# Applying a norm before or behind the products: scaled residual as the operand, the root multiplied into PSUM

## The chip, the core and the metric
One core of a Trainium2 chip (trn2) runs the whole program. The metric is the device time in microseconds of one execution, the median over several runs.

## The reference, cut to what matters
Two layers of a hybrid backbone on 640 tokens: 128 prompt tokens (columns 0 to 127) and 512 sample tokens, each group with its own modulation. Every layer is a mixer followed by a feed-forward part, and ahead of each stands a norm over the 1024 features:

```python
h = rms_norm(x) * P['norm_mix'][layer] * (1 + sc1) + sh1
x = x + g1 * mixer(h)
h = rms_norm(x) * P['norm_ffn'][layer] * (1 + sc2) + sh2
x = x + g2 * conv_ffn(h, ...)       # silu(a) * val of dwconv3(h @ w_up), then @ w_down
```

With gain = norm * (1 + sc) this is h = gain * x * r + sh, where r is one number per token. So h @ W = r * ((gain * x) @ W) + sh @ W. The feed-forward part has 2816 hidden features, a convolution over three neighbouring tokens (not across the two groups) and a bias. Layer 0 mixes by retention and a state-space scan, layer 1 by attention (qkv).

## The kernel before
Activations lie with features on the 128 partitions (eight tiles) and the 640 tokens as columns. A *unit* is one tile of 128 output features: its weights are loaded by SyncE into `raw` (four buffers), ScalarE rounds them to `w_hi` (`act_split`), and another engine makes `w_lo = raw - w_hi` (`low_split`). TensorE (`pe_tile`, L379) makes three products per tile of the contraction (w_hi with the high part, w_lo with the high part, w_hi with the low part of the operand), each in two halves of 320 columns: 48 products in a unit with eight tiles, 42 in one with seven. Two PSUM pairs (`pj`) alternate, and TensorE waits for the reading of the unit before the last (`pj_read0/1`) and for `w_lo`. `w_hi` and `w_lo` have two buffers each.

Each engine has its instructions in one written order, tied by semaphores. The stages in order: modulation A, dt, xs, bc, z, qk, v, g, wo_ssm, wo_ret, then for layer 0 up00, dn00, up01, dn01, up02, dn02 (16 up units and 8 down units, then 14 and 8 twice), kk, q, vv, attention, wo, and up10 to dn12.

Five norms: norm00, normS, norm01 (ahead of up00), norm10 (ahead of kk), norm11 (ahead of up10). All but normS are *wide*. For a wide norm ScalarE squares the tiles of x, VectorE adds them, TensorE sums over partitions (`pe_wide`, L684) with some filler products (`pe_keep`, L678), ScalarE takes the root (`act_root`, L730), VectorE the reciprocal (L742), TensorE spreads it over the partitions (`pe_spread`, L717). Then, tile by tile, VectorE multiplies x by gain and root (L773), ScalarE adds the shift and rounds to `h_hi` (L829), VectorE makes `h_lo` (L783). TensorE begins two units of the next stage interleaved in the order `SKEW`.

In an up unit ScalarE reads PSUM twice, into `u_sb` (L845) and, scaled and with bias, into `t_sb` (L846). VectorE adds the neighbours in two passes, each with a small piece across the chunk edges (L859, L860, L862, L863). Every second unit ScalarE takes the silu (L964), VectorE multiplies (`hf`, L980), ScalarE rounds to `hid_hi` (L966), VectorE makes `hid_lo` (L982). In a down unit VectorE adds the gated result to x (L895, three pieces), and in the last stage ahead of a norm the squares follow (L654, L664).

VectorE also computes the modulation vectors of the later stages in 80 units of four multiply-adds of 512 columns (L564, L567); behind every fourth stands a flip (two transposes L575, a reduce L577). Units 0 to 21 lie in qk to g, 22 to 27 in wo_ssm, 28 to 34 in wo_ret, and 35 to 79 in the feed-forward of layer 0: one behind every second up unit, three more in up01, one behind each unit of dn00 and dn01 and behind four of dn02.

Of the kernel before, what the change touches and what calls it, by code (L numbers as in the profile page):

```python
# [22 lines left out]
HALF = TOK // 2  # L23
COL = [0, 128, 256, 384, 512]
# [60 lines left out]
def build(nc, a, o):  # L85
# [55 lines left out]
    with ctx:  # L141
# [36 lines left out]
        hf2 = sb("hf2", [128, 2, TOK])  # L178
        u_sb = sb("u_sb", [128, 2, TOK])
# [94 lines left out]
        A = Region(A0, A_BYTES)  # L274
        Q2 = A("Q2", [128, AH, TOK], F32R)
# [15 lines left out]
        rope = Region(A0 + 65536, 2048)("rope", [128, 2, 4, 64])  # L291
# [79 lines left out]
        def pe_tile(pe, s, r, k, i, f, X, low=None, high=None):  # L371

            for n, (w, v) in enumerate(((w_hi, X[0]), (w_lo, X[0]), (w_hi, X[1]))):
                if n == 2 and low:
                    pe.wait_ge(*low)
                for hh in range(2):
                    if high and n == 0:
                        pe.wait_ge(*high[hh])
                    last = pe.matmul(pj(f)[:, hh, :], w[:, i % 2, k * 128:(k + 1) * 128], v[:, k, hh * HALF:(hh + 1) * HALF],  # L379
                                     start=(k == 0 and n == 0), stop=(k == s.K - 1 and n == 2))  # L380
            return last

        def pe_unit(pe, s, r, j, X, used=None):
# [5 lines left out]
            for k in range(s.K):  # L389
# [5 lines left out]
        SKEW = ((0, 0), (1, 0), (0, 1), (1, 1), (0, 2), (0, 3), (1, 2), (0, 4), (0, 5), (1, 3), (0, 6), (0, 7),  # L395
                (1, 4), (1, 5), (1, 6), (1, 7))

# [9 lines left out]
        def pe_first(pe, units, X, ready):  # L407
# [4 lines left out]
            elif ready[0] == "hid_ready":  # L412
                m = 4 if units[0][0].name[:3] == "dn0" else 2
                steps = [(0, k) for k in range(K - 1)] + [(1, k) for k in range(m)] + [(0, K - 1)] + [(1, k) for k in range(m, K)]
            else:
                steps = LATER if units[0][0].name == "wo_ssm" else SKEW
            for n, k in steps:
                s, r = units[n]
                if k == 0:
                    pe_begin(pe, s, r)  # L420
                low = high = None
                if n == 0:
                    low = (S(ready[0]), ready[1] + k + 1)
                    if ready[0] == "h_ready" and k == 0 and APPLIED[ready[1] // KT] in WIDE:
                        high = (S("h_hi_a"), WIDE.index(APPLIED[ready[1] // KT]) + 1), (S("h_hi"), ready[1] + 1)
                    elif ready[0] == "h_ready":
# [3 lines left out]
                last = pe_tile(pe, s, r, k, s.u0 + r, s.f0 + r, X, low, high)  # L430
# [21 lines left out]
        H, HID = (h_hi, h_lo), (hid_hi, hid_lo)  # L452
# [57 lines left out]
        def act_modA(act):  # L510
            for k in range(KT):
# [4 lines left out]
                if k == 6:  # L516
# [11 lines left out]
                    "modD": (48, 96, ((1, 0), (1, 1)))}  # L528
# [96 lines left out]
        WIDE = [p for p in NORMS if p != "normS"]  # L625
# [61 lines left out]
        def pe_wide(pe, name):  # L687
# [9 lines left out]
            if i:  # L697
                pe_keep(pe, flat[:, 2048:2560], (192,))
            pe.wait_ge(S("sq_a"), WIDE.index(name) + 1)
            pe_square_sum(pe, 0, sq[:, 1, :], False, True).then_inc(S("ms"), 1)  # L700
            if i:
                pe_keep(pe, flat[:, 2048:2560], (128,))
            pe.wait_ge(S("sq"), KT * (i + 1))
            pe_square_sum(pe, 1, sq[:, 1, :], False, True).then_inc(S("ms"), 1)
            if i:
                pe_keep(pe, flat[:, 2048:2560], (256,))

        def pe_spread(pe, name):
# [3 lines left out]
            if name in WIDE:  # L712
# [6 lines left out]
                if STEP0[name]:  # L719
                    pe_keep(pe, B6, (256, 128))  # L720
# [118 lines left out]

        def act_conv_in(act, s, r, j, cw):  # L840

            c = s.c0 + r
            if c >= 2:
# [3 lines left out]
                           scale=cw[:, r + 4 * j, 1:2] if isinstance(j, int) else cw[:, ds(r + 4 * j, 1), 1]).then_inc(tp_read(s, r), 1)  # L847

# [39 lines left out]
        PIECES = [(0, 0, 0, 128, 0), (1, 0, 128, HALF, 128), (1, 1, 0, HALF, HALF)]  # L888

        def dve_residual(dve, s, r, gate, first=False):  # L890
            evac_wait(dve, s, r, 0)
            out = pj(s.f0 + r)
            for g, hh, a0, a1, c0 in PIECES:
                xs_ = x[:, r, c0:c0 + a1 - a0]
                ins = dve.scalar_tensor_tensor(xs_, out[:, hh, a0:a1], gate(r, g), xs_, MUL, ADD)  # L895
                if first and g and not hh:
                    ins.then_inc(S("res_a"), 1)
            ins.then_inc(tp_read(s, r), 1)

        def act_out_stage(act, s, norm=None, hooks={}):  # L900
            for r in range(s.M):
# [14 lines left out]
        EARLY = 28  # L916
# [1665 lines left out]
```

## Time and profile before

| | |
|---|---|
| median of 3 runs | 1963.88 us (1961.39 to 1965.11) |
| profiled execution, first to last instruction | 1963.8 us |
| TensorE / VectorE / ScalarE / GpSimd busy | 97% / 65% / 42% / 6% |
| mean granted clock of TensorE | 0.994 |
| HBM read, mean rate | 170 MB, 89 GB/s |

Products overlap, so that a busy TensorE doesn't tell how fast it works: the distance of two starts does. A timeline row merges like instructions; in brackets is the engine's idle time just before and who ended it. A windows row gives, for each engine, busy time and count, then TensorE's granted clock, the DMA share and GB/s.

### The profile page before, as it was taken

The page shows a single profiled execution, that of the slowest core. Times are in us where ns is not written, and L with a number is a line of the kernel's source. Part 1 is how long each engine was busy: PE and PEld are TensorE (multiplying, and loading weights), DVE is VectorE, ACT ScalarE, POOL GpSimd, SP SyncE. Part 2 cuts the span into 40 slices and gives each one's busy share as a digit, 9 for nine tenths or more (in the row PEclk, how much of TensorE's full clock was granted, in tenths as well). Part 3 has the DMA queues.
Part 4 walks back from the last instruction along what each step waited for, and adds up shares of the span by engine and source line. Part 5 has one row for each costly group of instructions (what it writes and reads, how often), then busy time and mean ns, then how long its engine had stood idle before and what let it go on. Part 6 is the DMA issues. An engine that isn't in the chain of part 4 may idle for free.

```text
span 1963.8 us, 33247 instructions
## 1 busy us (share of the span) xinstructions
PE 1899.8 (97%) x13415; PEld 1803.0 (92%) x13415; DVE 1267.7 (65%) x2101; ACT 818.5 (42%) x1367; POOL 119.6 (6%) x106
## 2 busy tenths in 40 slices
PE   7999999999998999999999999899999999999999
PEld 4998799999988899999999989866698999999999
DVE  5555944666877878878978876656536553553553
ACT  4645743222444355234234345555525541441441
POOL 0000200000020000000000026411100000000000
PEclk9999999999999999999999999999999999999999
DMA  8221012445311333433433322100012222222222
GB/s 309 86 77 39 13 60 87 150 137 155 114 57 62 122 107 118 144 125 117 161 131 103 109 90 67 57 1 1 1 54 65 75 66 84 75 67 77 73 69 78
DMA packets 57066, 175.96 MB, mean 90 GB/s; under 512 B 7553, under 2 KB 9473, under 8 KB 56833
## 3 DMA queue, kind: packets, MB, share of 16 engines
q1 hardware_dynamic: 55152, 172.17, 27.3%
q10 hardware_dynamic: 1808, 2.36, 0.3%
q8 instruction: 69, 1.13, 0.3%
q14 instruction: 37, 0.30, 0.0%
HBM read 170.05 MB, written 4.46 MB: 89 GB/s over the span
## 4 chain that ended last, share of the span: by engine, by line
PE 83%; DVE 9%; ACT 4%; issue 2%; DMA 1%; POOL 1%; SPq 0%; ACTq 0%; DVEq 0%; POOLq 0%
PE ps L379 69%; PE ps L2117 2%; PE ps L2102 2%; DVE t_sb L773 1%; DVE w_lo L368 1%; DVE h_lo L783 1%; ACT w_hi L360 1%; PE ps L880 1%; PE ps L1295 1%; DVE PT L2234 1%; PE ps L2070 1%; PE ps L2069 1%; DVE x L895 1%; PE ps L1282 1%; DMA modw<-in_w_modA 1%
## 5 line engine op out<-in xcount | busy, mean ns | idle before, releaser
L379 PE MATMUL ps<-h_hi,w_hi 128*128 128x320 f32 x2768 | 638.6, 312 | 9.0 <-DVE w_lo L368 3.2
L379 PE MATMUL ps<-h_lo,w_hi 128*128 128x320 f32 x2768 | 633.7, 310 | 9.4 <-DVE h_lo L783 8.2
L379 PE MATMUL ps<-h_hi,w_lo 128*128 128x320 f32 x2768 | 630.8, 309 | 0.0
L368 DVE TENSOR_TENSOR w_lo<-raw,w_hi 128x1024 fp32r<-128x1024 f32 (+1 forms) x218 | 268.0, 1230 | 449.3 <-ACT w_hi L360 449.1
L360 ACT ACTIVATE w_hi<-raw 128x1024 fp32r<-128x1024 f32 (+1 forms) x221 | 230.7, 1044 | 694.1 <-PE ps L379 693.9
L379 PEld LDWEIGHTS ps<-h_lo,w_hi 128*128 128x128 f32 x2768 | 462.2, 188 | 16.5 <-DVE h_lo L783 14.9
L379 PEld LDWEIGHTS ps<-h_hi,w_hi 128*128 128x128 f32 x2768 | 461.1, 188 | 16.7 <-issue 5.2
L379 PEld LDWEIGHTS ps<-h_hi,w_lo 128*128 128x128 f32 x2768 | 463.4, 188 | 0.0
L379 PE MATMUL ps<-hid_hi,w_hi 128*128 128x320 f32 x704 | 161.7, 311 | 3.8 <-DVE x L895 2.8
L379 PE MATMUL ps<-hid_hi,w_lo 128*128 128x320 f32 x704 | 160.8, 309 | 0.0
L379 PE MATMUL ps<-hid_lo,w_hi 128*128 128x320 f32 x704 | 160.7, 309 | 0.0
L379 PEld LDWEIGHTS ps<-hid_hi,w_hi 128*128 128x128 f32 x704 | 117.8, 188 | 5.9 <-issue 2.6
L379 PEld LDWEIGHTS ps<-hid_hi,w_lo 128*128 128x128 f32 x704 | 118.3, 188 | 0.0
L379 PEld LDWEIGHTS ps<-hid_lo,w_hi 128*128 128x128 f32 x704 | 118.2, 188 | 0.0
L567 DVE SCALAR_TENSOR_TENSOR maccB<-mrawB,csil,maccB 128x512 f32<-128x512 f32 x168 | 115.3, 746 | 0.0
L895 DVE SCALAR_TENSOR_TENSOR x<-ps,modT,x 128x128 f32<-128x128 f32 (+2 forms) x216 | 81.3, 432 | 14.0 <-PE ps L379 14.0
L2089 DVE TENSOR_REDUCE nmax<-ps 128x1 f32<-128x640 f32 (+1 forms) x80 | 57.1, 715 | 38.1 <-PE ps L2070 38.0
L966 ACT ACTIVATE hid_hi<-hf 128x640 f32 (+1 forms) x44 | 32.6, 740 | 112.2 <-DVE hf L980 112.2
L846 ACT ACTIVATE t_sb<-ps,fconv 128x640 f32<-128x640 f32 x88 | 77.3, 878 | 0.0
L863 DVE SCALAR_TENSOR_TENSOR t_sb<-u_sb,fconv,t_sb 128x635 f32<-128x635 f32 x88 | 76.9, 874 | 0.0
L860 DVE SCALAR_TENSOR_TENSOR t_sb<-u_sb,fconv,t_sb 128x635 f32<-128x635 f32 x88 | 76.9, 874 | 0.0
L845 ACT ACTIVATE u_sb<-ps 128x640 f32<-128x640 f32 x104 | 71.5, 687 | 2.2 <-PE ps L379 2.2
(285 smaller groups left out, 2008.0 us busy)
## 6 DMA issues: line engine op xcount, KB each, us to landing
raw<-in_ffn_up SPq DMA_DIRECT2D x88, 512.0 KB, 3.6
raw<-in_hyb_in SPq DMA_DIRECT2D x49, 512.0 KB, 3.8
mrawB<-in_w_modB SPq DMA_DIRECT2D x48, 512.0 KB, 4.3
mrawA<-in_w_modB SPq DMA_DIRECT2D x64, 256.0 KB, 2.8
raw<-in_ffn_down SPq DMA_DIRECT2D x32, 448.0 KB, 3.3
raw<-in_hyb_out SPq DMA_DIRECT2D x16, 512.0 KB, 4.2
raw<-in_ffn_down SPq DMA_DIRECT2D x16, 512.0 KB, 3.5
modw<-in_w_modA SPq DMA_DIRECT2D x12, 512.0 KB, 13.2
```

What stands on the lines that cost most here:

```text
L360: act.activation(w_hi[:, i % 2, 0:n], raw[:, b % RAW, 0:n], ACT.Copy).then_inc(S("w_hi"), 1)
L368: eng.tensor_tensor(w_lo[:, i % 2, 0:n], raw[:, b % RAW, 0:n], w_hi[:, i % 2, 0:n].bitcast(F32), SUB).then_inc(S("w_lo"), 1)
L379: last = pe.matmul(pj(f)[:, hh, :], w[:, i % 2, k * 128:(k + 1) * 128], v[:, k, hh * HALF:(hh + 1) * HALF], start=(k == 0 and n == 0), sto ...
L567: ins = dve.scalar_tensor_tensor(acc, w, c, acc, MUL, ADD)
L845: act.activation(two(u_sb[:, r % 2, :]), pj(s.f0 + r), ACT.Copy).then_inc(S("cv_u"), 1)
L846: act.activation(two(t_sb[:, r % 2, :]), pj(s.f0 + r), ACT.Identity, bias=cw[:, r + 4 * j, 3:4] if isinstance(j, int) else cw[:, ds(r + 4 ...
L860: dve.scalar_tensor_tensor(t[:, :, 1:128], u[:, :, 0:127], w(0), t[:, :, 1:128], MUL, ADD).then_inc(S("cv_mid"), 1)
L863: dve.scalar_tensor_tensor(t[:, :, 0:127], u[:, :, 1:128], w(2), t[:, :, 0:127], MUL, ADD).then_inc(S("cv_done"), 1)
L895: ins = dve.scalar_tensor_tensor(xs_, out[:, hh, a0:a1], gate(r, g), xs_, MUL, ADD)
L2089: dve.tensor_reduce(nmax[:, n % 4:n % 4 + 1], score(n), AX.X, MAX, negate=True).then_inc(S("at_m"), 1)
L2102: last = pe.transpose(TP[:, b, :], Pr[n % 3][:, b * 128:(b + 1) * 128], ident)
L2117: last = pe.matmul((B6, B7)[u % 2][64 * par:64 * par + 64, 0:256].rearrange("p (m t) -> p m t", m=2), v, PT[:, u % 2, b - b0, par:AR:2, :] ...
```

## The change
For norm01, norm10 and norm11 the operand of the products becomes gain * x (high part by ScalarE in `act_scaled`, low part by VectorE in `dve_scaled`), made within the units of the stage ahead. The shifts of both groups are two extra columns (128 and 129), so operands have 642 columns, in pieces of 322 and 320; the hidden tiles keep these columns too. The sum over features is taken with one-column products (`pe_ms`) within the first unit and the root is spread within the second (`pe_spread` without its wide part); ScalarE copies it into `rstd` (`act_rstd`). VectorE multiplies each unit's PSUM by `rstd` (`dve_product`), ScalarE adds the shift column in two pieces (`act_shifted`) and then makes `up_t` from `up_u`; the convolution is two passes without small pieces. The two first units of a stage run one after the other. All `low_split` are VectorE's now. Four modulation units move from wo_ret to the z stage (EARLY 28 to 32); the modulation sums for layer 1 are split in two (modD, modE); the load of the retention state and some regions of SBUF move.

```diff
+        def act_scaled(act, name, k):
+            l, w = LAYER_OF[name]
+            for g, c0, c1, at in APART:
+                ins = act.activation(XS[name][0][:, k, at:at + c1 - c0], x[:, k, c0:c1], ACT.Copy, scale=gains[:, l, w, k, g:g + 1])
+            ins.then_inc(S("h_hi"), 1)
+        def dve_product(dve, s, r, j=0):
+            evac_wait(dve, s, r, j)
+            dve.wait_ge(S("prod_free"), PROD0[s.name] + r + 4 * j)
+            dve.tensor_tensor(prod[:, 0:2 * MID].rearrange("p (h c) -> p h c", h=2), pj(s.f0 + r, MID),
+                              rstd[:, 0:2 * MID].rearrange("p (h c) -> p h c", h=2), MUL).then_inc(tp_read(s, r), 1)
+        def act_shifted(act, s, r, j, out, to):
+            act.wait_ge(tp_read(s, r), (s.f0 + r) // 2 + 1 + 2 * j)
+            for (c0, c1), b, at in zip(((0, 128), (130, GAP)), (128, 129), to):
+                ins = act.activation(out[:, at:at + c1 - c0], prod[:, c0:c1], ACT.Identity, bias=prod[:, b:b + 1])
+            ins.then_inc(S("prod_free"), 1)
+        def act_up_in(act, s, r, j, cw):
+            c = s.c0 + r
+            act.wait_ge(S("cv_done"), c - 1 + 4 * j)
+            act_shifted(act, s, r, j, up_u[:, r % 2, :], (0, 130))
+            act.wait_ge(*shifted(s, r, j))
+            act.activation(up_t[:, r % 2, 0:GAP], up_u[:, r % 2, 0:GAP], ACT.Identity, bias=..., scale=...).then_inc(S("up_in"), 1)
+        def dve_up_conv(dve, s, r, j, cw):
+            c, p, n = s.c0 + r, r % 2, GAP - 1
+            dve.wait_ge(S("up_in"), c - stages["up00"].c0 + 1 + 4 * j)
+            u, t = up_u[:, p, :], up_t[:, p, :]
+            dve.scalar_tensor_tensor(t[:, 1:n + 1], u[:, 0:n], w(0), t[:, 1:n + 1], MUL, ADD).then_inc(S("cv_mid"), 1)
+            dve.wait_ge(S("cv_mid"), c + 1 + 4 * j)
+            dve.scalar_tensor_tensor(t[:, 0:n], u[:, 1:n + 1], w(2), t[:, 0:n], MUL, ADD).then_inc(S("cv_done"), 1)
...
             def body(r, j):
+                dve_product(dve, s, r, j)
                 low_split(dve, s.u0 + r + 2, j)
-                dve_conv(dve, s, r, j, cw)
+                dve_up_conv(dve, s, r, j, cw)
...
-        LATE = [("wo_ret", r) for r in range(7)]
+        LATE = [("wo_ret", r) for r in range(3)]
...
-            pe_wide(pe, "norm01")
-            pe_spread(pe, "norm01")
...
```

## Rows read from the trace of the kernel before

**Rows 1.** The page: busy times of the engines, and the chain by engine.
```profile
PE 1899.8 (97%) x13415; PEld 1803.0 (92%) x13415; DVE 1267.7 (65%) x2101; ACT 818.5 (42%) x1367; POOL 119.6 (6%) x106
...
PE 83%; DVE 9%; ACT 4%; issue 2%; DMA 1%; POOL 1%; SPq 0%; ACTq 0%; DVEq 0%; POOLq 0%
```
**Rows 2.** Timeline of ScalarE in up02: start, duration, instruction, idle before.
```profile
1067.74 1.06 ACT L360 ACTIVATE w_hi<-raw 128x1024 fp32r<-128x1024 f32 x1 [4.44 <-PE ps L379]
...
1070.06 0.74 ACT L964 ACTIVATE t_sb<-t_sb 128x640 f32<-128x640 f32 x1
...
1074.78 1.06 ACT L360 ACTIVATE w_hi<-raw 128x1024 fp32r<-128x1024 f32 x1 [0.71 <-PE ps L379]
```
**Rows 3.** Windows over norm01, norm10 and norm11, with two units behind each.
```profile
666.16:691.19 25.03, 22.05 (x170) 18.30 (x169) 19.56 (x43) 14.56 (x27) 2.37 (x1) 1.00 0.13 43
1149.61:1174.08 24.47, 21.96 (x171) 18.48 (x171) 20.34 (x44) 12.98 (x25) 2.36 (x1) 1.00 0.09 23
1483.60:1508.50 24.90, 21.97 (x171) 18.28 (x170) 19.34 (x40) 14.60 (x27) 2.36 (x1) 1.00 0.08 23
```
**Rows 4.** Windows within up01 and within up10.
```profile
857.00:954.00 97.00, 97.00 (x663) 97.00 (x662) 83.28 (x127) 40.27 (x54) 0.00 (x0) 1.00 0.39 126
1508.50:1560.00 51.50, 51.50 (x351) 51.50 (x352) 31.24 (x47) 28.04 (x34) 0.00 (x0) 1.00 0.26 82
```
**Rows 5.** Timeline of TensorE at the start of dn01 and dn02.
```profile
960.02 0.56 PE L379 MATMUL ps<-hid_hi,w_hi 128*128 128x320 f32 x2 [0.73 <-DVE x L895]
...
1110.19 0.67 PE L379 MATMUL ps<-hid_hi,w_hi 128*128 128x320 f32 x2 [2.06 <-DVE x L895]
1110.66 0.73 PE L379 MATMUL ps<-hid_hi,w_lo 128*128 128x320 f32 x2
```
**Rows 6.** Timeline of VectorE at the end of dn02 and in norm10.
```profile
1145.39 1.12 DVE L895 SCALAR_TENSOR_TENSOR x<-ps,modT,x 128x128 f32<-128x128 f32 x3
...
1155.05 1.00 DVE L773 SCALAR_TENSOR_TENSOR t_sb<-x,gains,ps 128x128 f32<-128x128 f32 x2
```
**Rows 7.** Timeline of TensorE around the sums of normS.
```profile
329.48 1.17 PE L672 MATMUL ps<-cst,ssq 128*128 128x1 f32 x10
330.51 0.54 PE L379 MATMUL ps<-h_hi,w_hi 128*128 128x320 f32 x2
```
**Rows 8.** Timelines: VectorE in the retention part, ScalarE in norm10.
```profile
556.69 0.81 DVE L1777 TENSOR_TENSOR PTr<-ps,mTf 128x640 f32<-128x640 f32 x1
...
1164.02 1.01 ACT L829 ACTIVATE h_hi<-t_sb,modT 128x128 fp32r<-128x128 f32 x2 [0.95 <-DVE t_sb L773]
```
**Rows 9.** Timeline of VectorE in an odd unit of up01.
```profile
877.00 1.22 DVE L368 TENSOR_TENSOR w_lo<-raw,w_hi 128x1024 fp32r<-128x1024 f32 x1
...
878.27 0.87 DVE L860 SCALAR_TENSOR_TENSOR t_sb<-u_sb,fconv,t_sb 128x635 f32<-128x635 f32 x1
879.18 0.23 DVE L862 SCALAR_TENSOR_TENSOR t_sb<-u_sb,fconv,t_sb 128x3 f32<-128x3 f32 x1
...
880.30 0.83 DVE L980 TENSOR_TENSOR hf<-t_sb 128x640 f32<-128x640 f32 x1
882.03 0.83 DVE L982 TENSOR_TENSOR hid_lo<-hf,hid_hi 128x640 fp32r<-128x640 f32 x1 [0.91 <-ACT hid_hi L966]
```
**Rows 10.** Timeline of VectorE in up01: a modulation unit with its flip.
```profile
868.77 2.73 DVE L567 SCALAR_TENSOR_TENSOR maccB<-mrawB,csil,maccB 128x512 f32<-128x512 f32 x4
...
873.89 1.22 DVE L368 TENSOR_TENSOR w_lo<-raw,w_hi 128x1024 fp32r<-128x1024 f32 x1
```
**Rows 11.** Windows behind two waits of TensorE.
```profile
1112.00:1116.00 4.00, 4.00 (x23) 4.00 (x23) 4.00 (x8) 0.74 (x1) 0.00 (x0) 0.77 0.61 220
...
1203.00:1208.00 5.00, 3.97 (x28) 3.97 (x29) 4.37 (x5) 1.59 (x3) 1.67 (x2) 1.00 0.34 107
```
**Rows 12.** Timeline of TensorE in the qkv stage.
```profile
1204.03 0.77 PE L1893 MATMUL ps<-cst,rt 128*128 128x128 f32 x5 [1.63 <-POOL rt L1884]
```
**Rows 13.** DMA issues: KB each, median us from issue to landing.
```profile
hf<-in_s_ret ACTq DMA_DIRECT2D x1, 512.0 KB, 5.4
```

More of the change, by code:

```diff
@@ L23 @@
 HALF = TOK // 2
+GAP = TOK + 2
 COL = [0, 128, 256, 384, 512]
@@ L405, in pe_begin, with pe_first @@
                 pe.wait_ge(S(f"pj_read{f % 2}"), f // 2)
-        def pe_first(pe, units, X, ready):
+        def pe_first(pe, units, X, ready, norm=None):
             K = units[0][0].K
@@ L414, in pe_first @@
                 steps = [(0, k) for k in range(K - 1)] + [(1, k) for k in range(m)] + [(0, K - 1)] + [(1, k) for k in range(m, K)]
+            elif norm:
+                steps = [(0, k) for k in range(K)] + [(1, k) for k in range(K)]
             else:
-                steps = LATER if units[0][0].name == "wo_ssm" else SKEW
+                steps = LATER
             for n, k in steps:
+                if norm and (n, k) == (0, 5):
+                    pe_ms(pe, norm, tp_base[norm])
+                if norm and (n, k) == (1, 1):
+                    pe_spread(pe, norm)
                 s, r = units[n]
@@ L450, in tp_full @@
             eng.wait_ge(S("tp_full"), t + 1)
-        H, HID = (h_hi, h_lo), (hid_hi, hid_lo)
+        HALVES = (0, HALF), (HALF, TOK)
+        MID = HALF + 2
+        H, ATTN = (h_hi, h_lo, HALVES), (ya_hi, ya_lo, HALVES)
+        XS = {p: t + (((0, MID), (MID, GAP)),) for p, t in (("norm01", (ya_hi, ya_lo)), ("norm10", (ya_hi, ya_lo)), ("norm11", (yh_hi, yh_lo)))}
+        HIDS = [t + (((0, MID), (MID, GAP)),) for t in ((yh_hi, yh_lo), (ya_hi, ya_lo))]
         QUARTER = (0, 2, 1, 3)
@@ new lines, in dve_scaled, with act_rstd @@
+        def dve_scaled(dve, name, k):
+            l, w = LAYER_OF[name]
+            dve.wait_ge(S("h_hi"), KT * APPLIED.index(name) + k + 1)
+            for g, c0, c1, at in APART:
+                ins = dve.scalar_tensor_tensor(XS[name][1][:, k, at:at + c1 - c0], x[:, k, c0:c1], gains[:, l, w, k, g:g + 1],
+                                               XS[name][0][:, k, at:at + c1 - c0].bitcast(F32), MUL, SUB)
+            ins.then_inc(S("h_ready"), 1)
+        def act_rstd(act, name):
+            act_root(act, name)
+            tp_full(act, tpf_base[name])
+            for g, c0, c1, at in APART:
+                ins = act.activation(rstd[:, at:at + c1 - c0], flat[:, 2048 + c0:2048 + c1], ACT.Copy)
+                if not g:
+                    continue
+                ins.then_inc(S("tp_read"), 1)
+            for at in (128, GAP):
+                ins = act.activation(rstd[:, at:at + 2], ones[:, 0:2], ACT.Copy)
+            ins.then_inc(S("prod_free"), 1)
@@ new lines, in build @@
+        PROD0, c = {}, 0
+        for n, names in enumerate((("up00", "up01", "up02"), ("kk", "q", "vv"), ("up10", "up11", "up12"))):
+            for t in names:
+                PROD0[t] = n + 1 + c
+                c += stages[t].M
+        def dve_product(dve, s, r, j=0):
[3 more added lines that the diff above has]
+                              rstd[:, 0:2 * MID].rearrange("p (h c) -> p h c", h=2), MUL).then_inc(tp_read(s, r), 1)
@@ L885, in dve_T, with pieces, dve_residual @@
             dve.tensor_copy(dst, TP).then_inc(S("tp_read"), 1)
-        PIECES = [(0, 0, 0, 128, 0), (1, 0, 128, HALF, 128), (1, 1, 0, HALF, HALF)]
-        def dve_residual(dve, s, r, gate, first=False):
+        def pieces(s):
+            at = 130 if s.name[:2] == "dn" else 128
+            return [(0, 0, 0, 128, 0), (1, 0, at, at + HALF - 128, 128), (1, 1, 0, HALF, HALF)]
+        def dve_residual(dve, s, r, gate):
             evac_wait(dve, s, r, 0)
-            out = pj(s.f0 + r)
-            for g, hh, a0, a1, c0 in PIECES:
+            out = pj(s.f0 + r, MID)
+            for g, hh, a0, a1, c0 in pieces(s):
                 xs_ = x[:, r, c0:c0 + a1 - a0]
                 ins = dve.scalar_tensor_tensor(xs_, out[:, hh, a0:a1], gate(r, g), xs_, MUL, ADD)
-                if first and g and not hh:
-                    ins.then_inc(S("res_a"), 1)
             ins.then_inc(tp_read(s, r), 1)
@@ L2448, in _ @@
             pool_ret(pool)
-            low_split(pool, stages["wo_ret"].u0 + 9)
             pool_tables(pool)
-            low_split(pool, stages["dn02"].u0 + 9)
             pool_rope(pool)
             pool_att(pool)
-            low_split(pool, stages["wo"].u0 + 9)
         @block.tensor
```

233 lines of the change are left out of this document (131 added, 102 removed).

## The prediction
> **What bounds the kernel now.** I read the page's busy shares first, then its chain, then three kinds of stretch. TensorE is busy 97% of the span, VectorE 65%, and the chain that ended last lies on TensorE for 83% and on VectorE for 9% [rows 1]. So a change gains only what it takes out of TensorE's queue or of TensorE's waits. Where it runs undisturbed a unit takes 7.04 us from one split of ScalarE to the next (1067.74 to 1074.78) [rows 2]: 48 products, 0.1467 us each.
>
> The reader is then to see two places. First, the borders: from the last product before a wide norm to the third unit behind it pass 25.03, 24.47 and 24.90 us [rows 3], in which TensorE has two units (14.08 us) of the new stage. 10.95, 10.39 and 10.82 us, 32.2 in all, are the norm: sums of squares, spread, kept-warm products, and waits of 0.8 us for h_lo. Second, the feed-forward of layer 0. There VectorE is nearly full already: 83.3 of 97.0 us between 857 and 954, against 31.2 of 51.5 in layer 1 [rows 4]. TensorE waited for it where up goes over into down: twice at dn01, 0.73 us each (the later stands), and 2.06 us at dn02 [rows 5].
>
> **The change, part by part.** I sum against the profiled execution, 1963.8 us from first to last instruction; the median of the runs is 1963.88, so no correction.
>
> *Borders.* Scaled residuals are made unit by unit, so only the last of eight tiles is late. After the last product at T: residual 1.12, square-add 0.8, scaling 1.0 like L773, square-add 0.8, scaling 1.0 on VectorE [rows 6], so the last h_lo comes at about T+4.8, and TensorE asks for it at T+7. The second unit's w_lo comes at about T+6 and is asked for at T+8. No wait is left. The old interleaving, pe_wide, pe_keep and the 16 spread products go. In their place come five sums (L672) and five spreads (L723), each five in 1.03 us up to the next product, 1.12 with that one's slower start, as L672 stands in the qk stage; the spread, which writes more columns, I take as the same [rows 7]: 2.24 per border, 6.7 in all. The product of unit 0 must wait for the root: spread at T+10.4, ScalarE's copies to T+11.8, product done T+12.7, w_lo of unit 2 T+13.9; TensorE wants both at T+16. Hidden with 2 us to spare. Net -32.2+6.7 = -25.5 (bounds -28 and -20: spread half as dear, or a wait of 2 us at each border).
>
> *Columns.* 2 more per pair of products, in 100 up and qkv units (24 pairs) and 48 down units (1056 pairs): 3456 pairs. A product is 0.1467 us for 320 columns, so at most 0.46 ns per column, at least 0.42 if part is fixed: +3.0 us (2.9 to 3.2).
>
> *Feed-forward, layer 0.* A product on VectorE comes ahead of every unit, and the convolution loses its two small pieces. The new thing is not the busy time but a relay: VectorE multiplies, ScalarE adds the shift in two pieces, waits for itself and makes up_t, and only then may VectorE convolve. Before, both ScalarE readings of PSUM could run ahead while VectorE was late. Costs: the product like PTr, 0.81; two ScalarE pieces (128 and 512) 1.01 from the first's start to the second's end; up_t like L964, 0.74 [rows 8, 2]. Hand-overs are 0.03 to 0.14 us: hid_hi and two of them fill 0.91 around its 0.74 [rows 9]; 0.05 each, with 0.08 for the wait on itself, is my estimate. From product to convolution 2.75 us. low_split (1.22, and 1.13 to the next start, since VectorE starts an instruction some 0.08 before the last one's end) fits inside and hides; 0.8 of the relay is idle. The convolution: 0.91 to its second half (878.27 to 879.18); that, 0.80 where nothing waits for it and 0.98 where the next waits for its end (1.12 from 879.18, less 0.14 for the small piece). Even unit: 2.75+1.71 = 4.5 us (was 1.13+0.14+0.91+0.14+0.80 = 3.1). Odd unit: 2.75+0.91+0.98, then 1.73 from hf to hid_lo, 0.75 for that = 7.1 us [rows 9]. A modulation unit adds 2.65 (2.73 less the 0.08); every fourth also the flip, 2.47, since both take 5.12 (868.77 to 873.89) [rows 10]. A pair with its modulation unit is 14.3 us; TensorE's pair is 14.08+0.04. VectorE had about 2.3 us to spare in a pair without flip and now has none.
>
> What lag L (VectorE's start on an even unit, behind TensorE's end of it) costs nothing? The w_lo of unit r+2 comes at L+2.1 and is wanted at 7.06, so L up to 4.9. After each pair L becomes max(7.06, L+4.5)+9.8-14.12, that is 2.7 from rest, and L+0.15 later; a flip adds 2.47. up00 (flips at r=1 and 9): 5.2 after the first pair, wait 0.3; three pairs at 0.13; second flip, wait 2.6. Sum 3.4, and 0.2 in dn00. up01 has three extra modulation units and three flips: VectorE needs about 117.8 us for what TensorE does in 98.8. Carried over the stage and dn01 by the same rule: waits of 0.4, 0.1, 2.7, 1.2, 2.7, then 2.9, 0.5 and 1.1 in dn01, sum 11.7. up02 and dn02: 0.9, then 1.0 and 3.6 at the start of dn02 (flip in the last pair), 0.1: 5.6. All: 20.9. The same carrying with the costs of before gives 0.9, 1.2 and 2.1 in the two down stages, 4.5 with small ones, against the measured 0.73, 0.73 and 2.06 [rows 5]; so the rule is trusted to about 0.3 per wait.
>
> *Clock.* Behind its wait of 2.06 us TensorE's first two products took 0.47 us and the next ones 0.53 per two, against 0.29, to 1113.9: at 1.2 instead of 2.4 GHz, 1.4 us lost, and a granted clock of 0.77 from 1112 to 1116. Behind 1.63 us at 1204 the clock stayed 1.00 [rows 5, 11, 12]. Five waits above are over 2 us: 5 x 1.4, against 1.4 before, +5.6; part is paid twice, since a late TensorE lets VectorE catch up, and the carrying has counted that within up01. Feed-forward 0: 20.9-4.5+5.6 = +22. Bounds: +3 if ScalarE's leg hid altogether (VectorE's busy time alone), +14 with 0.15 us less per relay, +29 with 0.2 us more.
>
> The Trainium skill (TensorE: Matmul & The Clock Gate, HAM oscillation) says that a kernel whose array waits again and again can be throttled anew behind each wait. [rows 11] agree for 2.06 us and not for 1.63; by that rule alone, with all waits over 1 us counted, the term would be about 5 us larger.
>
> *Feed-forward, layer 1.* No modulation units: pairs take 4.5+7.1 = 11.6 of 14.1 us. The hidden tiles come 0.1 us later for each down stage: +0.2.
>
> *QKV.* Product and wider ScalarE copy hide in the steady part. At its start TensorE already waits for the rope chain, 1.63 us at the third flip [rows 12]. Behind the K flips VectorE goes straight on, so each product (0.75) sits in that chain, three times: +2.5 us (0 to 6, the upper with a clock drop and a late start of attention).
>
> *At nothing, or nearly.* Four modulation units move into the z stage, where VectorE has a low_split, a product and a square-add, 1.2+0.8+0.8 us of each 7.04; 2.65 more fit, and the w_lo of the next unit stands ahead of them in the queue; their loads keep their distance of about three units. If that cover were gone a unit would cost 2.65. The state load moves two hooks later: issued at about 547.7 by my reckoning (7.04 us per unit, flip at r=5), landing 5.4 us later, first asked for ahead of the mask at 556.69; cover 3.6 us [rows 13, 8]. The two mod sums: one extra group on TensorE, +0.3. The POOL low_split leaves the border.
>
> Sum: -25.5+3.0+22+0.2+2.5+0.3 = +2.5, so **1966.3 us**.
>
> **The rivals.** *Relay overlaps (faster).* If ScalarE's leg falls under low_split or runs in less than I take, VectorE keeps its spare time in up01 and the waits stay near 3 to 10. For it: ScalarE is only 42% busy [rows 1], and 0.8 us of idle per relay decides all. Against it: the hand-overs in [rows 9] leave little to shave. Time: 1966.3-19 = 1947 to 1966.3-9 = 1957. It decides below 3.9 us per even unit.
> *VectorE costs more (slower).* The product reads two PSUM banks while ScalarE and TensorE use others; 0.2 us more per relay gives +7, a longer qkv chain +3, clock drops of 2 us instead of 1.4 +3: about 1979. It decides above 4.7 us per even unit.
> *The borders don't close.* A wait on the last scaled tile or the root of over 3 us each would leave 10 of the 25: 1976. Against it stands the slack of 2 us worked out above. This includes that the change fails to do its work.
>
> **How the numbers follow.** Forecast 0.55, with its own range 1959 to 1974; relay overlaps 0.20; VectorE dearer 0.17; borders 0.08. A measurement here can tell 0.2%, 3.9 us, from no change. Faster: 0.20 and 0.05 of the forecast's lower end, 0.25. Same: 0.30, all of it the forecast. Slower: 0.20 of the forecast's upper end with 0.17 and 0.08, 0.45. Range 1952 to 1984: it leaves out the lower half of the overlap case and the ends of the slower two.
>
> **What would show it.** Borders: from the last product to the third unit 16.3 us, instead of 25. up00, up01 and up02: TensorE waiting for w_lo (low_split) with single waits of 2.5 to 3 us behind flips, most in up01, VectorE over 95% busy or in short waits for ScalarE there, product to convolution 2.75 us. Layer 1: no waits, unit 7.06 us. Granted clock below 1.00 behind the long waits. Wrong if up01 shows less than 5 us of waits, if its relay is under 2.3 us, or if TensorE waits at the borders.

## The result and the profile after

The changed kernel takes 1983.85 us (median of 5, 1982.65 to 1986.82), the kernel before in the same session 1965.11 (1961.39 to 1966.03): ratio 1.0114, 95% interval 1.0102 to 1.0125. It is slower: by 19 us between these two medians, by 22 us by the ratio (the kernel before took 1961.6 to 1961.9 beside most later runs). I had forecast 1966.3, no measurable change, though I had given "slower" the largest chance, 0.45; the time lies at the very end of the range. The profiled execution spans 1985.0 us, 21.2 more than that of before.

The page of the changed kernel, busy times and the chain by engine (answers to [rows 1]):

```profile
PE 1904.7 (96%) x13261; PEld 1814.5 (91%) x13261; DVE 1303.7 (66%) x1986; ACT 865.4 (44%) x1476; POOL 114.0 (6%) x103
...
PE 71%; DVE 14%; ACT 8%; issue 6%; DMA 1%; POOL 1%; ACTq 0%; SPq 0%; DVEq 0%; POOLq 0%
```

VectorE's and ScalarE's share of the chain has grown from 13% to 22% and "issue" from 2 to 6: somewhere TensorE now follows these two. Where, the distance between equal marks tells. ScalarE splits the weights of the same 221 units in both kernels, and each split (but for the first two of a stage) starts when TensorE is done with the unit two before. Taking the start of each split in both traces gives how much each stage grew:

| stretch | growth, us | by the prediction |
|---|---|---|
| all up to wo_ret's last units | +0.1 | +0.3 |
| three borders | -8.40, -8.09, -8.09: -24.6 | -25.5 |
| up00 / dn00 | +8.70 / +0.45 | layer-0 stages in all: |
| up01 / dn01 | +18.11 / 0.00 | +22, and |
| up02 / dn02 | +6.52 / +2.31 | columns of 1.4: |
| these six | +36.1 | +23.4 |
| qkv with attention | +3.9 | +2.8 |
| wo | +0.6 | 0 |
| layer 1, feed-forward | +4.8 | +1.6 |
| first split and rounding | +0.3 | |

The borders, TensorE from the first product on gain * x to that of the third unit; the three rows answer to [rows 3]:

```profile
666.21:682.69 16.48, 16.48 (x118) 16.48 (x117) 8.49 (x15) 7.99 (x14) 0.00 (x0) 1.00 0.23 69
1177.35:1194.32 16.97, 16.97 (x124) 16.96 (x122) 8.61 (x15) 6.56 (x15) 0.00 (x0) 1.00 0.17 52
1507.74:1524.20 16.46, 16.46 (x119) 16.46 (x117) 8.34 (x15) 7.99 (x14) 0.00 (x0) 1.00 0.13 37
```

16.3 had been forecast; TensorE is busy throughout. What is left of the norm stands in TensorE's timeline as two groups of small products, 1.03 us each to the next product, as taken from [rows 7]:

```profile
670.69 1.17 PE L682 MATMUL ps<-cst,ssq 128*128 128x1 f32 x10
671.72 0.54 PE L387 MATMUL ps<-ya_hi,w_hi 128*128 128x322 f32 x2
...
675.34 1.28 PE L720 MATMUL ps<-cst,rs 128*128 128x128 f32 x10
676.37 0.54 PE L387 MATMUL ps<-ya_hi,w_hi 128*128 128x322 f32 x2
```

The loss lies in the feed-forward of layer 0. All that TensorE waited for between 679 and 1180 us (waits view: engine, line, who ended the wait; us in total, times, longest):

```profile
PE ps L387 <- DVE w_lo L375: 19.9, 12, 4.2
PE ps L387 <- DVE x L995: 4.5, 2, 3.9
PE ps L387 <- DVE yh_lo L1094: 1.0, 2, 0.5
```

That is 25.4 us, against 4.1 in these stages before. The largest, in TensorE's timeline:

```profile
760.66 0.56 PE L387 MATMUL ps<-ya_hi,w_hi 128*128 128x322 f32 x2 [3.00 <-DVE w_lo L375]
...
909.69 0.63 PE L387 MATMUL ps<-ya_hi,w_hi 128*128 128x322 f32 x1 [2.74 <-DVE w_lo L375]
927.14 0.56 PE L387 MATMUL ps<-ya_hi,w_hi 128*128 128x322 f32 x2 [1.61 <-DVE w_lo L375]
944.20 0.56 PE L387 MATMUL ps<-ya_hi,w_hi 128*128 128x322 f32 x2 [2.52 <-DVE w_lo L375]
...
968.74 0.90 PE L387 MATMUL ps<-yh_hi,w_hi 128*128 128x322 f32 x2 [4.19 <-DVE w_lo L375]
...
1137.77 0.66 PE L387 MATMUL ps<-yh_hi,w_hi 128*128 128x322 f32 x2 [3.86 <-DVE x L995]
```

VectorE in two units of up01 that follow one another (start, duration; the last row begins the next unit). It answers to [rows 9]:

```profile
907.60 0.82 DVE L898 TENSOR_TENSOR prod<-ps,rstd 128x644 f32<-128x644 f32 x1
908.34 1.22 DVE L375 TENSOR_TENSOR w_lo<-raw,w_hi 128x1024 fp32r<-128x1024 f32 x1
910.74 0.89 DVE L938 SCALAR_TENSOR_TENSOR up_t<-up_u,fconv,up_t 128x641 f32<-128x641 f32 x1 [1.18 <-ACT up_t L928]
911.66 0.89 DVE L940 SCALAR_TENSOR_TENSOR up_t<-up_u,fconv,up_t 128x641 f32<-128x641 f32 x1
912.46 0.82 DVE L898 TENSOR_TENSOR prod<-ps,rstd 128x644 f32<-128x644 f32 x1
...
915.54 0.89 DVE L938 SCALAR_TENSOR_TENSOR up_t<-up_u,fconv,up_t 128x641 f32<-128x641 f32 x1 [1.13 <-ACT up_t L928]
...
919.20 0.83 DVE L1094 TENSOR_TENSOR yh_lo<-up_m,yh_hi 128x642 fp32r<-128x642 f32 x1 [0.91 <-ACT yh_hi L1073]
919.94 2.73 DVE L581 SCALAR_TENSOR_TENSOR maccB<-mrawB,csil,maccB 128x512 f32<-128x512 f32 x4
```

From product to convolution pass 3.14 and 3.08 us, and VectorE stands idle for 1.18 and 1.13 of them. An even unit is 4.86 us (907.60 to 912.46), an odd one 7.48 (912.46 to 919.94). The forecast had 2.75, 4.5 and 7.1. ScalarE's side of the same kind of relay shows where the difference is:

```profile
881.27 1.02 ACT L905 ACTIVATE up_u<-prod 128x128 f32<-128x128 f32 x2 [1.67 <-DVE prod L898]
882.54 0.93 ACT L928 ACTIVATE up_t<-up_u,fconv 128x642 f32<-128x642 f32 x1 [0.24 <-ACT up_u L905]
```

up_t takes 0.93 us and not the 0.74 of L964, which has neither scale nor bias vector, and ScalarE stands idle for 0.24 us behind its own shift and not 0.08. A row of the right form stood in the trace of the kernel before, just ahead of the one that I took (ScalarE in up02):

```profile
1069.29 0.88 ACT L846 ACTIVATE t_sb<-ps,fconv 128x640 f32<-128x640 f32 x1
```

It reads PSUM and not SBUF, but has scale and bias as vectors, and takes 0.88 us. The Trainium skill (ScalarE: Activation LUTs, What ACT_TABLE_LOAD costs) gives 186 ns and 0.833 ns per element for an instruction with immediate scale and bias, and about 93 ns more for each of the two that is a vector. My estimate from these figures is 0.91 us for up_t; the row shows 0.93.

### The profile page after: what moved, and what is told of

The parts are those of the page before. It is cut to its first block, busy times and chain, and to the rows that moved or that the text cites. A ratio compares the mean times of both kernels' runs of the same rounds, so it can differ in the third digit from the quotient of the medians.

```text
span 1985.0 us, 33178 instructions
## 1 busy us (share of the span) xinstructions
PE 1904.7 (96%) x13261; PEld 1814.5 (91%) x13261; DVE 1303.7 (66%) x1986; ACT 865.4 (44%) x1476; POOL 114.0 (6%) x103
## 4 chain that ended last, share of the span: by engine, by line
PE 71%; DVE 14%; ACT 8%; issue 6%; DMA 1%; POOL 1%; ACTq 0%; SPq 0%; DVEq 0%; POOLq 0%
PE ps L387 58%; PE ps L2221 2%; PE ps L2236 2%; ACT up_t L928 2%; DVE maccB L581 2%; ACT up_u L905 2%; DVE up_t L938 2%; DVE prod L898 2%; DVE up_m L1092 1%; DVE up_t L940 1%; PE ps L978 1%; PE ps L2189 1%; DVE PT L2353 1%; ACT yh_hi L1073 1%; PE ps L1407 1%
## 5 line engine op out<-in xcount | busy, mean ns | idle before, releaser
L387 PE MATMUL ps<-ya_hi,w_hi 128*128 128x322 f32 (+1 forms) x1376 | 321.3, 315 | 16.0 <-DVE w_lo L375 15.0
L387 PE MATMUL ps<-ya_hi,w_lo 128*128 128x322 f32 (+1 forms) x1376 | 317.2, 312 | 0.0
L387 PE MATMUL ps<-ya_lo,w_hi 128*128 128x322 f32 (+1 forms) x1376 | 316.7, 312 | 0.0
L387 PE MATMUL ps<-yh_hi,w_hi 128*128 128x322 f32 (+1 forms) x1056 | 244.3, 312 | 10.5 <-DVE w_lo L375 4.9
L387 PEld LDWEIGHTS ps<-ya_hi,w_hi 128*128 128x128 f32 x1376 | 231.1, 190 | 20.7 <-issue 18.7
L387 PE MATMUL ps<-h_hi,w_hi 128*128 128x320 f32 x1040 | 241.8, 314 | 7.3 <-DVE w_lo L375 2.8
L387 PE MATMUL ps<-h_lo,w_hi 128*128 128x320 f32 x1040 | 238.4, 310 | 2.5 <-DVE h_lo L780 1.3
L387 PE MATMUL ps<-h_hi,w_lo 128*128 128x320 f32 x1040 | 237.7, 310 | 0.0
L387 PEld LDWEIGHTS ps<-h_hi,w_hi 128*128 128x128 f32 x1040 | 173.2, 189 | 12.2 <-DVE w_lo L375 4.9
L387 PEld LDWEIGHTS ps<-h_lo,w_hi 128*128 128x128 f32 x1040 | 174.4, 189 | 3.8 <-DVE h_lo L780 2.2
L387 PEld LDWEIGHTS ps<-h_hi,w_lo 128*128 128x128 f32 x1040 | 174.5, 189 | 0.0
```

Source lines behind the costliest of these rows:

```text
L387: last = pe.matmul(pj(f, c1 - c0)[:, hh, :], w[:, i % 2, k * 128:(k + 1) * 128], v[:, k, c0:c1], start=(k == 0 and n == 0), stop=(k == s.K ...
```

## The experiments

**Is it the idle time or the work?** VectorE's relays in layer 0 hold 47.9 us of idle time (43 of the 44 units read from the timeline), while its modulation work waits behind them. The first kernel moves that work into the gaps.

```diff
+            def fill(r, room):            # pieces of modulation units, in their order
+                while todo and room > 0 and todo[0][0] <= r + 1:
+                    room -= todo[0][1]
+                    todo.pop(0)[2]()
             def body(r, j):
                 dve_product(dve, s, r, j)
                 low_split(dve, s.u0 + r + 2, j)
+                fill(r, 2)
                 dve_up_conv(dve, s, r, j, cw)
...
+                    fill(r, 1)
                     dve.wait_ge(S("hid_hi"), p + 1 + 2 * j)
...
-                if l == 0:
-                    dve_late(dve, s, r)
+                due(r if r == s.M - 1 else r - 1)
```

> In the up stages of layer 0 the pieces of the modulation units (multiply-adds, transposes, reduce) are written into the places where VectorE waits for ScalarE: up to two behind each low_split, one between hf and hid_lo, at most one unit earlier than now; what is left is done at most one unit later. Nothing else changes. Relay theory (the +36 us of the layer-0 feed-forward are VectorE standing idle for ScalarE's leg, about 1.15 us in every unit and 0.9 in every odd one, on top of a full load): up01 needs 120.3 us of VectorE today, 98 with 14 x 1.15 and 7 x 0.9 filled, against 99.5 of TensorE; up00 and up02 have room to spare. The stalls nearly vanish; of 36 us 5 to 10 stay (4 of them columns): time 1953 to 1960, below the kernel before. Busy-time theory (VectorE's own instructions are slower or contended, the idle is only where the waiting shows): filling gains under 8 us, time 1977 to 1985.

Measured: 1953.82 us (1952.17 to 1956.28), ratio to the kernel before 0.9959 (0.9946 to 0.9973). The relay theory's forecast came true in size: the six stages grew by 2.6 us in place of 36.1, up01 by 0.33 in place of 18.11. VectorE in up01 of this kernel, timeline:

```profile
898.81 0.83 DVE L934 TENSOR_TENSOR prod<-ps,rstd 128x644 f32<-128x644 f32 x1
899.90 1.22 DVE L375 TENSOR_TENSOR w_lo<-raw,w_hi 128x1024 fp32r<-128x1024 f32 x1 [0.26 <-ACT w_hi L367]
901.04 1.41 DVE L579 SCALAR_TENSOR_TENSOR maccB<-mrawB,csil,maccB 128x512 f32<-128x512 f32 x2
902.37 0.88 DVE L974 SCALAR_TENSOR_TENSOR up_t<-up_u,fconv,up_t 128x641 f32<-128x641 f32 x1
903.28 0.89 DVE L976 SCALAR_TENSOR_TENSOR up_t<-up_u,fconv,up_t 128x641 f32<-128x641 f32 x1
```

Two multiply-adds stand where it stood idle, and the convolution follows at once. Over the six stages (windows: length, TensorE, its loads, VectorE, ScalarE, GpSimd, granted clock) VectorE's instructions and busy time are the same in both kernels, the changed one first and this one second, and only the length differs:

```profile
678.91:1180.32 501.41, 475.82 (x3135) 469.61 (x3134) 403.46 (x556) 205.37 (x278) 12.14 (x19) 0.98 0.35 116
```
```profile
680.58:1148.89 468.31, 464.69 (x3135) 462.84 (x3134) 403.39 (x556) 205.49 (x279) 12.15 (x19) 1.00 0.39 124
```

(Both run from the third split of up00 to the second of kk.) VectorE was 80% busy in the first, and that was too much; it is 86% busy in the second, and that is not. TensorE's waits in this stretch of the second are 3.6 us, all at down units:

```profile
PE ps L387 <- DVE x L1031: 3.6, 3, 2.0
```

**Without the modulation work.** The same question from the other side, in both kernels:

```diff
+            nc_ = 512 if i < 35 or r == 0 else 16
...
-                    w = mrawB[:, i % 2, k * 512:(k + 1) * 512]
+                    w = mrawB[:, i % 2, k * 512:k * 512 + nc_]
```

> The changed kernel, with the multiply-adds of modulation units 35 to 79 (layer-0 feed-forward) cut from 512 to 16 columns, except in the first unit of each four; that part of the modulation is left out, loads, transposes and reduces stay. Relay theory: pairs take 12.3 us plus small pieces against 14.2 of TensorE, so only flips can still make it wait, and little: layer-0 feed-forward grows by about 6 instead of 36 us over the kernel before, time about 1954. If stalls come from the units themselves or from the up-to-down borders and not from the sum with the modulation work: 1965 or more.

> The kernel before with the same part left out. Its three waits at dn01 and dn02 (3.5 us) and the drop of the clock behind one of them (1.4) go: 1959. So with the modulation thinned in both, the change should be worth about -5 us (borders -25, columns +10, qkv +4, rest +6), where it is worth +20 with it.

Measured: 1954.43 (ratio 0.9961, 0.9949 to 0.9973) and 1959.46 (0.9989, 0.998 to 0.9998); the six stages grow by 3.7 us over those of the kernel before in the first and shrink by 4.5 in the second. So the change by itself is worth -5 us where VectorE has room, and the modulation work turns that into +22. The kernel fill, which does all that work, is as fast as the one without it.

**How the time hangs on the relay.** Two lengthen it and one shortens it:

```diff
             act.wait_ge(*shifted(s, r, j))
+            if s.name[:3] == "up0":           # dose: one; dose2: three, to a scratch tile
+                act.activation(warm[:, :], eps, ACT.Copy)
```
```diff
-            act_shifted(act, s, r, j, up_u[:, r % 2, :], (0, 130))
-            act.wait_ge(*shifted(s, r, j))
-            act.activation(up_t[:, r % 2, 0:GAP], up_u[:, r % 2, 0:GAP], ...)
+            act.activation(up_t[:, r % 2, 0:GAP], prod[:, 0:GAP], ...)
+            act_shifted(act, s, r, j, up_u[:, r % 2, :], (0, 130))
...
             dve.wait_ge(S("up_in"), c - stages["up00"].c0 + 1 + 4 * j)
+            dve.wait_ge(*shifted(s, r, j))
```

> The changed kernel with one more ScalarE instruction of 0.2 us (128x1) in the relay of each of the 44 up units of layer 0, between the shift and up_t. Relay theory: VectorE has no spare time in these stages, so nearly each 0.2 us is paid: +6 to +9 us and 1 or 2 from the clock, 1991 to 1996. If the relay hides behind something: no change, 1984.

> The changed kernel with three more ScalarE instructions of 0.2 us (128x1) in the relay of each of the 44 up units of layer 0. In the run dose one such instruction fitted into the 0.25 us that ScalarE waits for its own shift, and the relay stayed at 3.09 us; so three lengthen it by about 0.37. Relay theory: VectorE has no spare time from the second pair of up00 to the end of up02, so 30 to 40 of 44 are paid: +11 to +16 us, a ratio of 1.017 to 1.020 to the kernel before instead of 1.0114. If only VectorE's own busy time counted: no change.

> The changed kernel with up_t made straight from prod, ahead of the two shift pieces, so that ScalarE doesn't wait for itself; what is left out is the shift in the centre tap of the convolution. The relay becomes shorter by 0.25 us (2.88 instead of 3.13). Relay theory: the same slope downward, -7 to -10 us, about 1975 (ratio 1.006 to 1.008). If only VectorE's own busy time counted: no change.

All three moved the way that was expected and each by less; the edits also changed the relay by less than I had reckoned. A small instruction on ScalarE fits into its 0.24 us of idle time, and three small ones take 0.39 us together, not 0.6. In dose the small instruction starts 0.03 us after the shift ends (884.16 after 884.13), though it stands behind the same wait as up_t in the changed kernel; so what the 0.24 us are made of is not shown. ScalarE in dose2:

```profile
898.69 1.02 ACT L906 ACTIVATE up_u<-prod 128x128 f32<-128x128 f32 x2 [4.32 <-DVE prod L899]
899.74 0.39 ACT L931 ACTIVATE more<-cst 128x1 f32<-128x1 f32 x3
900.03 0.91 ACT L932 ACTIVATE up_t<-up_u,fconv 128x642 f32<-128x642 f32 x1
```

Read from the traces (mean time from product to convolution over the up units of layer 0 but the first, and the growth of the six stages over the kernel before):

| kernel | relay, us | growth, us | ratio of the times |
|---|---|---|---|
| short | 3.01 | 32.6 | 1.0101 (1.0084 to 1.0118) |
| changed | 3.09 | 36.1 | 1.0114 (1.0102 to 1.0125) |
| dose | 3.11 | 36.6 | 1.0132 (1.0117 to 1.0148) |
| dose2 | 3.18 | 40.8 | 1.0154 (1.0137 to 1.0171) |

8.2 us for 0.17 us of relay: 48 us per us, about once for each of the 44 units. By this slope the 0.34 us that I had taken too little is 16 us. The growth from the changed kernel to dose alone is too small to carry weight, the steps are not even, and the intervals of neighbours overlap; the two ends, whose intervals don't, carry the reading.

**What a column costs.** Where nothing waits, units of the changed kernel take 7.10 to 7.13 us and not the 7.06 that two more columns should make of 7.04. ScalarE's splits in dn10, start to start, in the kernel before and in the changed one:

```profile
1642.67 1.06 ACT L360 ACTIVATE w_hi<-raw 128x1024 fp32r<-128x1024 f32 x1 [5.98 <-PE ps L379]
1649.71 1.06 ACT L360 ACTIVATE w_hi<-raw 128x1024 fp32r<-128x1024 f32 x1 [5.98 <-PE ps L379]
```
```profile
1652.73 1.06 ACT L367 ACTIVATE w_hi<-raw 128x1024 fp32r<-128x1024 f32 x1 [6.07 <-PE ps L387]
1659.87 1.06 ACT L367 ACTIVATE w_hi<-raw 128x1024 fp32r<-128x1024 f32 x1 [6.07 <-PE ps L387]
```

Five kernels ask whether length or place does it. b324 and b336 are the kernel before with one longer piece; pad and pad336 are the changed kernel with other places; fill320 is fill with short pieces.

```diff
-    last = pe.matmul(pj(f)[:, hh, :], w..., v[:, k, hh * HALF:(hh + 1) * HALF], ...)
+    c0, c1 = ((0, 324), (320, 640))[hh]          # b324; 336 in b336; not in a stage's first units
+    last = pe.matmul(ps[:, 2 * (f % 2) + hh, 0:c1 - c0], w..., v[:, k, c0:c1], ...)
```
```diff
-    ya_hi, ya_lo: [128, KT, GAP]
+    ya_hi, ya_lo: [128, KT, 656]                 # pad
-    MID = HALF + 2
+    MID = 336                                    # pad336, with pad
```

> The kernel before with products of 324 and 320 columns instead of 320 and 320, in all units that are not first of a stage; both start where they did (tiles keep their stride of 640), and the 4 more columns are never read. Columns theory (a product costs by its columns): 24 pairs x 4 x 0.42 ns = 0.04 us per unit, 7.08 instead of 7.04. If a product whose length isn't a multiple of 64 bytes pays more than its columns, as units of the changed kernel seem to (7.10 to 7.13 with 2 more columns): 7.12 or more.

> The kernel before, products of 336 and 320 columns (336 is a multiple of 64 bytes as 320 is), the 16 more never read. If a column costs 0.42 ns and only odd lengths are punished: 7.04 + 24 x 16 x 0.42 ns = 7.20 us per unit. If a column costs 1.04 ns, as 324 showed (7.14): 7.44.

> The changed kernel with the tiles of ya_hi and ya_lo 656 columns apart instead of 642, a multiple of 64 bytes; yh stays at 642 and serves as the control. Placement theory (the surplus over 0.42 ns per column comes from where a tile starts): a unit on ya goes from 7.13 to 7.09 or less and all its tiles take the same time, a unit on yh stays at 7.10. If length alone decides: no change in either.

> As pad, and all pieces are (0, 336) and (336, 642), so that on ya both pieces start on 64 bytes; VectorE's product reads 672 columns instead of 644. Placement theory: a unit on ya 7.06, what the columns alone cost. If only the tile's start counts: as pad. Time: the longer product costs about 0.03 us in the full VectorE of layer 0, 1 to 2 us there.

> The kernel fill, with every product 320 columns long (0 to 319, and 322 to 641 of tiles that stay 642 columns apart); two tokens' products are left out. Length theory: units go back to 7.04 and 6.16 us, the surplus of 0.06 to 0.10 per unit and most of the waits at the ups' ends go: about 1953.8 - 10 = 1944 (1942 to 1946). Placement theory (tiles start anywhere relative to 64 bytes, and that costs): units stay at 7.08 or more, time 1949 or more.

A steady unit of dn10 in each, from splits of consecutive units (b324, then b336):

```profile
1671.90 1.06 ACT L360 ACTIVATE w_hi<-raw 128x1024 fp32r<-128x1024 f32 x1 [6.09 <-PE ps L380]
1679.05 1.06 ACT L360 ACTIVATE w_hi<-raw 128x1024 fp32r<-128x1024 f32 x1 [6.09 <-PE ps L380]
```
```profile
1675.94 1.06 ACT L360 ACTIVATE w_hi<-raw 128x1024 fp32r<-128x1024 f32 x1 [6.14 <-PE ps L380]
1683.14 1.06 ACT L360 ACTIVATE w_hi<-raw 128x1024 fp32r<-128x1024 f32 x1 [6.14 <-PE ps L380]
```

| kernel | pieces | unit of dn10, us | columns alone would give |
|---|---|---|---|
| before | 320, 320 | 7.04 | |
| b336 | 336, 320 | 7.20 | 7.20 |
| b324 | 324, 320 | 7.15 | 7.08 |
| changed | 322, 320, tiles 642 apart | 7.13 | 7.06 |
| pad | 322, 320, tiles 656 apart | 7.15 | 7.06 |
| pad336 | 336, 306, tiles 656 apart | 7.09 | 7.06 |
| fill320 | 320, 320, tiles 642 apart | 7.07 | 7.04 |

Sixteen more columns cost 0.16 us, exactly 24 x 16 x 0.42 ns; four more cost 0.11, of which 0.04 is columns. In b324 nothing but the length differs from the kernel before, so there length alone makes a surplus of 0.07 us per unit. Aligned tiles alone (pad) don't help; with tiles 642 apart a piece of 320 still pays 0.03. But length is not all. The 306 columns of pad336 are no multiple of 16 (64 bytes) either, and its surplus is 0.03. In the changed kernel the same two lengths cost 7.13 and 6.25 us per unit on the tiles ya (dn10, dn11) and 7.10 and 6.20 on the tiles yh (up10, dn01), where the columns alone would give 7.06 and 6.18. What makes the surplus besides the length stays open. In time: b324 1984.99, b336 1991.16, pad 1983.36, pad336 1987.87, each one run, with 1961.6 to 1961.9 for the kernel before beside them. fill320 takes 1947.34 us (0.9928, 0.9912 to 0.9945), 6.5 less than fill, where I expected 10: units on ya went from 7.13 to 7.07 us, those on yh only from 7.10 to 7.09 (up10), and I had counted the surplus for both.

**The chain in qkv.** The last run tries to take the new work out of the norm and rope chain:

```diff
+                if 1 <= i < 10:
+                    chain(i - 1)
                 act_shifted(act, s, r, 0, sT3[:, i % 2, :], (0, 128))
                 if i >= 10:
                     act_split(act, s.u0 + r + 2)
-                if i >= 1:
-                    chain(i - 1)
+                    chain(i - 1)
```

> The kernel fill, and in qkv ScalarE squares the turned tile of the unit before (the start of the norm and rope chain) ahead of the shift of this one, for units 0 to 9. Chain theory (of the 4.4 us that qkv grew, what isn't columns, 3.7, is the new work of product and shift standing in that chain behind the K flips, 0.83 and 1.02 us at a time): the reduce starts when low_split ends, 0.8 us earlier, and two or three waits of TensorE shrink by as much: qkv +2 to +3 instead of +4.4, time 1951 to 1953. If the waits come from VectorE's flips alone: no change, 1953.8.

Measured: 1951.34 us (1949.76 to 1955.67), ratio 0.9938 (0.9924 to 0.9951). But the trace doesn't bear the expectation out: qkv grew by 4.28 us over the kernel before, against 4.38 in fill (both to a mark one unit earlier than in the table of stages; the changed kernel has 4.38 there too). GpSimd's part of the chain ends TensorE's waits in both, 3.5 us in 4 waits here and 2.8 in 2 in fill:

```profile
PE ps L2062 <- POOL rt L2051: 3.5, 4, 1.8
```

The chain theory as I put it fails: starting it earlier moved the waits and did not shorten them. The interval overlaps that of fill, and the difference of 2.5 us is not shown to be the edit's. Both kernels beat the kernel before.

## Why the prediction was wrong

**Borders**: right, -24.6 for -25.5 (-24.5 by the windows against [rows 3]). No wait came in at them, and the sums and spreads cost what [rows 7] said.

**Feed-forward, layer 0**: the mechanism was right. TensorE waits for w_lo behind the flips, most of it in up01 and dn01, and where the rule put them: in up01 and dn01 I had 0.4, 0.1, 2.7, 1.2, 2.7, 2.9, 0.5 and 1.1; the timeline has 0.62, 2.74, 1.61, 2.52, 0.24, 4.19 and 0.69. The step that failed is a duration: "From product to convolution 2.75 us" measured 3.09, and with it "even unit 4.5" and "odd unit 7.1" measured 4.86 and 7.48. It went wrong because I gave up_t the 0.74 us of a form without vectors (0.93 measured), and the wait of ScalarE on itself 0.08 us as an estimate where 0.24 us pass. The stages grew by 36.1 and not by 22 and 1.4 for columns; by the slope of the relay runs 0.34 us is more than enough for that, and my bound "+29 with 0.2 us more" points the same way.

Added up on TensorE's side the miss has more than one part. Its idle time grew by 21.3 us (25.4 less 4.1) where I had 16.4, the clock took 7.0 for 5.6, and the columns about 3.8 for 1.4 (0.06 us in each of 52 units, 0.04 in 16). A wait also costs more than its idle time, which I had left out: around the one of 3.00 us two products start 3.30 us apart and the next two 0.25, where 0.15 is usual, so 0.25 us more; sixteen waits in place of five make that 2.8 us. These sum to 34.9 of the 36.1. They are not independent, for whatever slows TensorE gives VectorE time; that the single waits came out so near to the forecast, with a relay 0.34 us too short in it, may owe something to that. One figure of the working is a slip: by its own durations VectorE needs 115.1 us in up01 (seven pairs of 11.6, ten modulation units, three flips) and not 117.8.

The rival "VectorE costs more" was to decide above 4.7 us per even unit and gave 1979: it is the case that came, with a chance of 0.17. Its reason was not the one I gave (two PSUM banks; the product takes the 0.82 us that I had), but ScalarE's leg. That leg was listed in the forecast as a quantity that decides all, and I gave its longer side 0.17.

**Clock**: the size was nearly right, and in part by luck. Granted clock of slices of 20 us in the changed kernel, behind the waits of 3.00, 2.74, 2.52, 4.19 and 1.95 us and the last of 3.86:

```profile
755.00:775.00 20.00, 17.00 (x115) 16.69 (x113) 16.56 (x21) 9.57 (x13) 0.00 (x0) 1.00 0.23 79
900.00:920.00 20.00, 17.26 (x107) 17.00 (x106) 15.00 (x19) 9.89 (x14) 0.00 (x0) 0.91 0.41 131
940.00:960.00 20.00, 17.25 (x115) 16.73 (x114) 15.52 (x20) 9.01 (x14) 0.00 (x0) 1.00 0.30 96
960.00:980.00 20.00, 15.12 (x84) 14.59 (x84) 17.08 (x25) 6.04 (x8) 0.00 (x0) 0.83 0.37 107
1060.00:1080.00 20.00, 18.05 (x111) 17.79 (x111) 16.53 (x21) 8.40 (x13) 0.00 (x0) 0.91 0.28 100
1120.00:1140.00 20.00, 15.65 (x104) 14.88 (x103) 16.71 (x27) 8.70 (x14) 0.00 (x0) 0.95 0.39 122
1140.00:1160.00 20.00, 20.00 (x133) 20.00 (x132) 19.26 (x33) 7.95 (x13) 0.00 (x0) 0.96 0.25 77
```

The shares missing from 1.00, times 20 us, are 8.8 us, against 1.8 before (0.91 between 1105 and 1125): +7.0 for +5.6. Behind the wait of 2.74 us two products take 0.53 us (910.92 to 911.45), the lower level of 1.2 GHz, until 912.5. "All waits over 2 us" was not the rule: behind 3.00 and 2.52 us the clock stayed, behind 1.95 it fell. Nor does the length of a wait alone decide. At the start of dn01 TensorE waits 1.98 us in fill and 1.99 in fillq, and the clock held in the first and fell in the second:

```profile
940.00:960.00 20.00, 18.02 (x122) 17.75 (x121) 18.24 (x28) 6.14 (x8) 0.00 (x0) 1.00 0.40 141
```
```profile
940.00:960.00 20.00, 18.02 (x111) 17.75 (x111) 19.52 (x30) 6.02 (x8) 0.00 (x0) 0.91 0.38 133
```

**Columns**: mis-sized. "At most 0.46 ns per column" held for 16 more columns (b336) and not for these. Steady up units take 0.06 us more, down units of layer 1 0.09 and those of dn01 0.04: 9 us in all where I had 3.0, though in up00 to up02 a part of it lies under VectorE's time.

**Feed-forward, layer 1**: no waits within the up stages, as forecast, but 4.8 us for 1.6. By TensorE's own marks, from its third unit (1508.50 and 1524.20) to the end, it is 5.5. Columns make 4.7 of that (42 up units at 0.06, 24 down units at 0.09). The other 0.8 are two waits for the last hidden tile, 0.25 us in dn11 and 0.54 in dn12 (`ya_lo`), where I had 0.1 us per down stage. That the longer relay delays that tile is argued and not shown.

**QKV**: +3.9 for +2.8; with columns taken at 0.06 per unit what remains is about 3.2 for 2.5. The size is near, but my reason for it (three products standing in the rope chain) is not shown, and the one run on it, fillq, didn't bear it out.

The terms that missed sum to the miss: 12.7 in the feed-forward of layer 0, 3.2 in that of layer 1, 1.1 in qkv, 0.9 at the borders and 0.6 in wo are 18.5 of the 18.7 us between the predicted time and the span (1966.3 and 1985.0).

## What to carry to other kernels

An engine that is 80% busy can be the bound: where its instructions wait for another engine's leg, count busy time and idle legs together, and look for independent work that can be written into the leg. Here that alone took 30 us and turned a loss of 1.1% into a gain of 0.4%. For a leg that occurs in every unit, take each duration from a row of the same form (same operands, scale and bias), since an error is multiplied by the number of units. Two columns more can cost as much as eight (0.09 us per unit in dn10), so time a new length before a change rests on it.

## What the runs showed of the hardware that I had not expected

A fp32r product costs 0.42 ns for each column added in sixteens (320 to 336: +6.7 ns), and 324 columns cost 4.6 ns more than 320 where 1.7 would be their share (0.11 us in 24 products). ScalarE issues three 128x1 instructions in 0.39 us, though each shows as 0.20, and one put between the shift and up_t delays up_t by only 0.02 us, since 0.24 us were idle there. TensorE's clock fell behind a wait of 1.95 us and held behind one of 3.00, and behind the same wait of 2.0 us it fell in one run and held in another.
